# RWKV-7 recurrence on one core: TensorE's turns, low-rank products and opening sum in 64x64 tiles, two factor products on GpSimd, the last inverse level added in PSUM

## The reference

```python
def step(s, inp):
    rt, wt, kt, vt, at, bt = inp
    sa = jnp.einsum('bhvk,bhk->bhv', s, at)
    s = s * wt[:, :, None, :] + sa[..., None] * bt[:, :, None, :] + vt[..., None] * kt[:, :, None, :]
    y = jnp.einsum('bhvk,bhk->bhv', s, rt) if return_y else None
    return s, y
```

## Time and profile before

| | us |
|---|---|
| median of 3 runs (lowest, highest) | 1623.71 (1621.64, 1624.52) |
| the profiled execution's own time | 1622.61 |
| its span | 1620.3 |
| TensorE busy, 14229 matmuls | 1455.2 (90%) |
| VectorE busy | 684.0 (42%) |
| ScalarE busy | 414.0 (26%) |
| GpSimd busy | 194.7 (12%) |
| TensorE's granted clock, mean | 0.957 of full |

### The profile page before, as it was taken

One profiled execution on the slowest core, in us unless ns is written; L12 is line 12 of the kernel. 1 busy time (PEld: TensorE's weight loads), 2 busy tenths in 40 slices (PEclk: granted clock), 3 DMA queues, 4 the chain that ended last, 5 costly groups with the idle time before them and its releaser, 6 DMA issues. The chain is left out here.

```text
span 1620.3 us, 32201 instructions
## 1 busy us (share of the span) xinstructions
PE 1455.2 (90%) x14229; PEld 829.2 (51%) x14229; DVE 684.0 (42%) x1310; ACT 414.0 (26%) x922; POOL 194.7 (12%) x216
## 2 busy tenths in 40 slices
PE   7999999799999998978999997791999988988985
PEld 4445657475554554767788885351333322322331
DVE  3121025554504926756666666286121222221224
ACT  3220135362200004545454553011110000000003
POOL 1100001310001111013333354000000000000000
PEclk9999999999999997989999999895999999999998
DMA  7455430320322111000000000815799999999991
GB/s 274 157 213 205 172 117 2 90 84 14 118 79 78 52 52 52 2 2 4 4 4 5 4 5 2 338 51 202 306 427 426 427 427 427 428 427 428 427 428 75
DMA packets 50731, 285.01 MB, mean 176 GB/s; under 512 B 3993, under 2 KB 7321, under 8 KB 37793
## 3 DMA queue, kind: packets, MB, share of 16 engines
q1 hardware_dynamic: 46592, 266.15, 40.7%
q0 software_dynamic: 2704, 10.18, 1.8%
q10 hardware_dynamic: 1296, 6.62, 1.0%
HBM read 276.63 MB, written 6.29 MB: 175 GB/s over the span
## 5 line engine op out<-in xcount | busy, mean ns | idle before, releaser
L1294 PE MATMUL PS<-arena 128*64 128x512 f32 x336 | 160.3, 632 | 28.7 <-issue 28.7
L1296 PE MATMUL PS<-arena 128*64 128x512 f32 x336 | 156.1, 612 | 0.0
L760 PE MATMUL PS<-arena,ring 128*128 128x512 f32 (+1 forms) x368 | 127.6, 509 | 0.0
L1294 PEld LDWEIGHTS PS<-arena 128*64 128x64 f32 x336 | 47.6, 145 | 130.8 <-issue 130.5
L704 PE MATMUL PS<-ring,arena 128*128 128x512 f32 (+1 forms) x256 | 109.8, 587 | 2.8 <-DMA ring<-w_in 1.5
L1080 PE MATMUL PS<-arena 64*64 64x64 f32 x3776 | 92.9, 224 | 10.8 <-DVE arena L1365 3.9
L798 ACT ACTIVATE arena<-PS 128x512 f32<-128x512 f32 (+3 forms) x76 | 34.7, 485 | 253.4 <-PE PS L760 112.6
L760 PEld LDWEIGHTS PS<-arena,ring 128*128 128x128 f32 x368 | 69.8, 190 | 57.7 <-issue 54.0
L626 DVE TENSOR_REDUCE arena<-PS 128x1 f32<-128x768 f32 (+4 forms) x96 | 62.7, 655 | 82.8 <-PE PS L534 35.4
L1080 PEld LDWEIGHTS PS<-arena 64*64 64x64 f32 x3776 | 77.8, 135 | 24.9 <-issue 9.2
L2387 DVE TENSOR_TENSOR arena<-PS,arena 64x512 f32<-64x512 f32 x32 | 22.0, 689 | 158.4 <-PE PS L1316 158.1
(11 more groups left out here) (361 smaller groups left out, 2609.5 us busy)
## 6 DMA issues: line engine op xcount, KB each, us to landing
arena<-exp_w_gate SPq DMA_DIRECT2D x21, 2048.0 KB, 30.1
arena<-exp_w_up SPq DMA_DIRECT2D x21, 2048.0 KB, 30.0
ring<-exp_w_down SPq DMA_DIRECT2D x20, 2048.0 KB, 31.1
ring<-w_ada SPq DMA_DIRECT2D x12, 2048.0 KB, 12.9
arena<-exp_w_down SPq DMA_DIRECT2D x12, 2048.0 KB, 30.7
ring<-exp_w_gate SPq DMA_DIRECT2D x11, 2048.0 KB, 31.0
ring<-exp_w_up SPq DMA_DIRECT2D x11, 2048.0 KB, 29.5
ring<-w_in SPq DMA_DIRECT2D x9, 2048.0 KB, 14.9
```

Of the source, the lines that this page charges most:

```text
L760: mm = pe.matmul(bank(b, 0, n), u[:, k, (i % 4) * P:(i % 4) * P + P], hT[:, k, t0:t0 + n], start=(k == 0), stop=(k == KT - 1))
L1294: pe.matmul(bank(c, 0, 512, (0, 64)), x, unit(u)[:, k, c * 512:c * 512 + 512], start=(n == 0 and k == 0), stop=(n == 1 and k == 3))
L1296: mm = pe.matmul(bank(c, 0, 512, (64, 128)), x, unit(u + 1)[:, k, c * 512:c * 512 + 512], start=(n == 0 and k == 0), stop=(n == 1 and k == 3))
```

## The change

1. turned() makes 16 matmuls of 64x64 against the 64x64 identity instead of four transposes of 128x128, through the four corners. The row copies bkN change their layout for it.
2. lora: each product of 128 output rows becomes two of 64.
3. The opening: two bf16 matmuls 128x128 by 256 columns become four of 64x64 by 256.
4. al and rt move from VectorE to GpSimd, al ahead of bt, rt ahead of kdk; wc goes to the end of GpSimd's list.
5. xt4 is added onto the turned X in PSUM (bank pair 3) instead of going to bank pair 2. XTf becomes a copy on ScalarE. far goes to bank pair 3, so an waits for Zm4 of the chunk before instead of FT.
6. vN gets a second buffer, and TensorE's, VectorE's and ScalarE's lists have a new order; the loop bodies follow them.

```diff
 SCAN_STEP = {
     "pe": (
-        ("R1b", 0), ("an", 1), ("ab", 1), ("U0", 0), ("tX0", 1), ("Z1", 1), ("U1", 0), ("x1", 1),
-        ("rows", 1), ("Z2", 1), ("tX1", 1), ("dS1", 0), ("dS2", 0), ("x2", 1), ("lora", 2),
-        ("Z3", 1), ("tX2", 1), ("y1", 0), ("x3", 1), ("ak", 1), ("tX3", 1), ("Z4", 1), ("y2", 0),
-        ("vnT", 1), ("y3", 0), ("xt4", 1), ("tL", 1), ("R1a", 1), ("far", 1),
+        ("an", 1), ("ab", 1), ("R1b", 0), ("Z1", 1), ("tX0", 1), ("rows", 1), ("x1", 1), ("U0", 0),
+        ("Z2", 1), ("tX1", 1), ("lora", 2), ("x2", 1), ("vnT", 1), ("U1", 0), ("Z3", 1), ("tX2", 1),
+        ("ak", 1), ("tL", 1), ("x3", 1), ("dS1", 0), ("dS2", 0), ("tX3", 1), ("Z4", 1), ("y1", 0),
+        ("y2", 0), ("y3", 0), ("xt4", 1), ("R1a", 1), ("far", 1),
     ),
     "dve": (
-        ("X0", 1), ("Zm1", 1), ("xa1", 1), ("Zm2", 1), ("xa2", 1), ("Sadd", 0), ("Smul", 0),
-        ("sga", 2), ("Zm3", 1), ("aa", 2), ("ssg", 2), ("xa3", 1), ("scan", 2), ("Zm4", 1),
-        ("Ark", 1), ("Aak", 1), ("yd", 0), ("XTf", 1), ("al", 2), ("FT", 1), ("rt", 2),
+        ("X0", 1), ("Zm1", 1), ("xa1", 1), ("Zm2", 1), ("sga", 2), ("xa2", 1), ("aa", 2), ("ssg", 2),
+        ("Zm3", 1), ("scan", 2), ("xa3", 1), ("Sadd", 0), ("Zm4", 1), ("Aak", 1), ("Ark", 1),
+        ("yd", 0), ("Smul", 0), ("FT", 1),
     ),
     "act": (
-        ("R1", 0), ("AbT", 1), ("U", 0), ("XT0", 1), ("ArbT", 1), ("U1e", 0), ("rowe", 1),
-        ("XT1", 1), ("XT2", 1), ("tsg", 2), ("ta", 2), ("XT3", 1), ("Ei", 2), ("vn", 1), ("ya", 0),
-        ("Ev", 2), ("L", 1), ("kf", 2),
+        ("AbT", 1), ("ArbT", 1), ("R1", 0), ("XT0", 1), ("rowe", 1), ("XT1", 1), ("U", 0),
+        ("tsg", 2), ("vn", 1), ("ta", 2), ("XT2", 1), ("U1e", 0), ("L", 1), ("Ei", 2), ("Ev", 2),
+        ("XT3", 1), ("kf", 2), ("ya", 0), ("XTf", 1),
     ),
     "pool": (
-        ("ArbM", 0), ("bts", 2), ("btk", 2), ("bt", 2), ("wc", 2), ("kdk", 2), ("kd", 2),
+        ("ArbM", 0), ("bts", 2), ("btk", 2), ("al", 2), ("bt", 2), ("rt", 2), ("kdk", 2), ("kd", 2),
+        ("wc", 2),
     ),
...
             def opened_by_unit():
 
-                for q in range(2):
-                    lo = pcol(2, q, 0)
-                    pe.matmul(PS[:, lo:lo + 256], unit_half, rep(outweigh_half, 4), start=True, stop=True,
-                              skip_group_check=True)
-
-            def turned(b, half, src, opens=True):
-
-                for d in range(2):
-                    for j2 in range(2):
-                        lo = pcol(b, d, half) + j2 * P
-                        mm = pe.matmul(PS[:, lo:lo + P], src(d, j2), ident, is_transpose=True, start=(opens and j2 == 0), stop=True,
-                                       skip_group_check=True)
+                for c in range(2):
+                    for r in range(2):
+                        lo, rows = pcol(2, r, 0), slice(r * 64, r * 64 + 64)
+                        pe.matmul(PS[c * 64:c * 64 + 64, lo:lo + 256], unit_half[rows, rows],
+                                  rep(outweigh_half[rows, :], 4), start=True, stop=True, skip_group_check=True)
+
+            def turned(b, half, src, frm, to):
+
+                begun = set()
+                for j, q, d in heads(frm, to):
+                    r = half_other(frm, j, q)[0]
+                    i, o = half_other(to, j, q)
+                    lo = pcol(b, o, half) + (2 * d + j // 2) * 64
+                    mm = pe.matmul(PS[i * 64:i * 64 + 64, lo:lo + 64], src(d, j, q),
+                                   C("ident2", 0, 64, (r * 64, r * 64 + 64)),
+                                   start=(o, i) not in begun, stop=True, skip_group_check=True)
+                    begun.add((o, i))
                 return mm
...
-                        pe.matmul(bank(0, c, 64), lora[0:64, d, j * P:j * P + P], wal[0:64, tok:tok + 64],
-                                  start=True, stop=True)
-                        mm = pe.matmul(bank(1, c, 64), lora[64:128, d, j * P:j * P + P], wal[64:128, tok:tok + 64],
-                                       start=True, stop=True)
+                        for h in range(2):
+                            lo, to = j * P + h * 64, (h * 64, h * 64 + 64)
+                            pe.matmul(bank(0, c, 64, to), lora[0:64, d, lo:lo + 64], wal[0:64, tok:tok + 64],
+                                      start=True, stop=True)
+                            mm = pe.matmul(bank(1, c, 64, to), lora[64:128, d, lo:lo + 64], wal[64:128, tok:tok + 64],
+                                           start=True, stop=True)
...
-                    signal(product(2, 0, A, A, split(W["Z"], A), whole(W["XT"], A), by_direction=True), "xt4", near)
...
+                    signal(product(3, 0, A, A, split(W["Z"], A), whole(W["XT"], A), clear="no"), "xt4", near)
...
+                if runs("al", ahead):
+                    needs(pool, ("Ei", ahead), ("an", ahead - 3), ("ak", ahead - 3), ("R1b", ahead - 3))
+                    signal(removal(pool, ahead), "al", ahead)
```

More of the change, by code:

```diff
@@ L68 @@
  FINAL) = range(17)
-N_SCAN = 27
+N_SCAN = 28
 LIVES = [
@@ L1138, in rwkv_pe @@
                 now, near, ahead = g, g + 1, g + 2
-                if runs("R1b", now):
-                    needs(pe, ("R1a", now), ("al", now), ("Smul", now - 1))
-                    signal(product(1, 0, A, A, al_of(now), split(W[f"S{now % 2}"], A), clear="no"), "R1b", now)
                 if runs("an", near):
-                    needs(pe, ("al", near), ("bt", near), ("FT", near - 1))
+                    needs(pe, ("al", near), ("bt", near), ("Zm4", near - 1))
                     opened_by_unit()
@@ L1172, in rwkv_pe @@
                     needs(pe, ("xa1", near), ("XT0", near))
-                    signal(turned(3, 0, pairs_of(W["X"])), "tX1", near)
-                if runs("dS1", now):
-                    needs(pe, ("rowe", now), ("vn", now), ("U1e", now))
-                    signal(product(1, 0, B, A, row_op(now, 1), whole(W["vN"], B), clear="bank"), "dS1", now)
-                if runs("dS2", now):
-                    needs(pe, ("U1e", now))
-                    signal(product(1, 0, B, A, row_op(now, 0), split(W["U"], B), clear="no"), "dS2", now)
+                    signal(turned(3, 0, whole(W["X"], B), B, A), "tX1", near)
+                if runs("lora", ahead):
+                    needs(pe, ("rowe", ahead - 1))
+                    signal(lora_products(ahead), "lora", ahead)
                 if runs("x2", near):
@@ L1182, in rwkv_pe @@
                     signal(product(2, 0, A, B, whole(W["XT"], A), split(W["Z"], A)), "x2", near)
-                if runs("lora", ahead):
-                    needs(pe, ("rowe", ahead - 1))
-                    signal(lora_products(ahead), "lora", ahead)
+                if runs("vnT", near):
+                    needs(pe, ("XT1", near))
+                    signal(turned(3, 0, values_of(near), A, B), "vnT", near)
+                if runs("U1", now):
+                    needs(pe, ("U", now), ("FT", now))
+                    signal(product(1, 1, B, B, split(W["FT"], B), split(W["U"], B), clear="no"), "U1", now)
                 if runs("Z3", near):
@@ L1410, in rwkv_dve @@
                     needs(dve, ("x1", near), ("X0", near))
[L1411 removed]
+                    x = of_blocks(W["X"])
                     signal(dve.tensor_tensor(x, x, pair4(2), ALU.add), "xa1", near)
@@ L1445, in rwkv_dve @@
                     signal(running_sums(), "scan", ahead)
+                if runs("xa3", near):
+                    needs(dve, ("x3", near), ("xa2", near))
+                    x = of_blocks(W["X"])
+                    signal(dve.tensor_tensor(x, x, pair4(2), ALU.add), "xa3", near)
+                if runs("Sadd", now):
+                    needs(dve, ("dS2", now), ("y1", now - 1), ("Smul", now - 1))
+                    signal(dve.tensor_tensor(both(f"S{(now + 1) % 2}"), both(f"S{now % 2}"), pair(1, 0), ALU.add), "Sadd", now)
                 if runs("Zm4", near):
@@ L1842, in _ @@
                     signal(act.activation(both("R1"), pair(1, 0), ACT.Copy), "R1", now)
-                if runs("AbT", near):
-                    needs(act, ("ab", near), ("Z4", near - 1), ("tL", near - 1))
-                    signal(act.activation(W["AbT"].rearrange("p (s q n) -> p q s n", q=2, n=64), pair_wide(0, 0), ACT.Copy), "AbT", near)
+                if runs("XT0", near):
+                    needs(act, ("tX0", near), ("xt4", near - 1))
+                    signal(act.activation(of_blocks(W["XT"]), pair4(3), ACT.Copy), "XT0", near)
+                if runs("rowe", near):
+                    needs(act, ("rows", near), ("dS2", near - 2))
+                    for a in range(2):
+                        ins = act.activation(of_blocks(row_half(near, a)), pair4(0, a), ACT.Copy)
+                    signal(ins, "rowe", near)
+                if runs("XT1", near):
+                    needs(act, ("tX1", near), ("x1", near))
```

(22 more changed lines are left out.)

224 lines of the change are left out of this document (103 added, 121 removed).

## The result

| | before | changed |
|---|---|---|
| median (lowest, highest), us | 1624.12 (1621.64, 1625.65) | 1695.5 (1694.29, 1696.61) |
| profiled execution's own time / its span | 1622.61 / 1620.3 | 1696.6 / 1694.8 |
| ratio, with its 95% interval | | 1.0436 (1.0423 to 1.0448) |
| TensorE busy, granted clock | 1455.2, 0.957 | 1443.5, 0.953 |
| VectorE, ScalarE, GpSimd busy | 684.0, 414.0, 194.7 | 653.3, 420.9, 212.0 |

The prediction was 1597 us, in a range of 1588 to 1611: wrong in sign. TensorE's busy time does fall by 12 us over the launch, and yet the launch takes 71 us more.

The account below looks back on a forecast made before the run. TensorE's work was taken to bound the recurrence: -27.1 us from first opening to last R1b and +0.5 at the start, -26.6 from 1622.6, gave 1596.0; with 1.1 for the median, 1597 us, range 1588 to 1611.

Parts of the forecast that it names:

- TensorE is the bound: Recurrence, 725 to 980 us: TensorE is busy 239 of 255 us at full clock, so its work sets the time.
- The prices of the array work: TensorE, latent step: a turn 0.52 for 0.70 us, low-rank products 1.04 for 2.04; 2.35 us less work in all.
- The rival of the 1.00 turn: Turns overlapping at two corners only cost 1.00 us each, 46 us above the sum: 1643 us; chance 0.07.
- the 0.87: Turn price in us if column tiling excludes the f32 transpose mode; 34 us above the sum, 1631 us.
- So 20.1 against 22.5: Recurrence: each of six latent steps takes 20.1 us instead of 22.5, 2.4 us less.
- The walk: New order laid on TensorE operation by operation with operand waits: latent step 20.1 us, context step 18.5.
- instructions arrive too slowly: Rival, recurrence: TensorE wants about 97 instructions a microsecond; if it got only 80, 1638 us; chance 0.03.
- the row against it: 907.8 to 918.5 us: 69 instructions a microsecond with TensorE busy 10.4 of 10.7 us, cited against slow instruction arrival.
- the 14.9 us of "issue" on L1080: 70 stalls on TensorE in the kernel before, cited for the rival of slow instruction arrival.
- The first rival: GpSimd or VectorE operands come 0.5 to 1.2 us late each step: +6 to +14 us, 1603 to 1611; chance 0.14.
- The order: TensorE's new order in a latent step leaves waits of 0.47 us before Z2 and 0.3 before far.
- I am wrong if ... 'issue' idle time grows by more than 10 us: Sign of failure on TensorE, beside turns over 0.8 us or TensorE waiting for GpSimd.

Follow-up runs that it names:

- a3: Changed kernel with 128x128 transposes, wide low-rank products and two-matmul opening put back; new order, GpSimd's al and rt, xt4 in PSUM stay: 1641.94 us, ratio 1.0088.
- a4: a3 plus seven f32 matmuls of 512 columns to an unused bank ahead of the first opening: 1637.29 us, ratio 1.0073 to the kernel before.
- c2: Kernel before with 256 already satisfied semaphore waits written for each step on SyncE: 1623.2 us, ratio 0.999.
- c1: Kernel before with 32 already satisfied semaphore waits written at eight places of a step on TensorE: 1709.56 us, ratio 1.0538.
- d1: Kernel before with 126 one-column bf16 matmuls added to each step on TensorE, into unused PSUM columns: 1659.61 us, ratio 1.0228.
- b2: Kernel before with seven f32 matmuls of 512 columns to an unused bank ahead of the first opening: 1626.35 us, ratio 1.0013.
- b3: Kernel before with only al and rt moved to GpSimd, in the changed kernel's order there: 1625.31 us, ratio 1.001.

## Why the prediction was wrong

**"TensorE is the bound": half right.** The array was busy 94% of the recurrence. But the instruction supply stood right behind it, at 21.4 us a latent step against 22.5, and was not costed as a bound of its own. By the 3.7 us a step could take an estimated 778 matmuls in its 22.5 us before its supply took over; the change asked for 996.

**The prices of the array work: right.** TensorE's timeline of the changed kernel, where no block ends:

```profile
915.89 1.62 PE L1125 MATMUL PS<-arena 64*64 64x64 f32 x96
...
920.39 0.69 PE L1104 MATMUL PS<-arena 64*64 64x64 f32 x32 [0.31 <-DVE arena L1423]
920.90 0.65 PE L1125 MATMUL PS<-arena 64*64 64x64 f32 x32
921.37 0.23 PE L1153 MATMUL PS<-arena 64*64 64x64 f32 x2
```

Three turns (tX0 and the double rows) take 915.89 to 917.36, 0.49 each, and tX1 at 920.90 takes 0.47; I had 0.52. The rival of the 1.00 turn is out, and so is the 0.87 worked out from the Trainium skill's rule on the transpose mode (TensorEngine Tiling, Restrictions and Gotchas; TensorE: Matmul & The Clock Gate, Terms) as a price of the turn. The low-rank products take 0.99 in the six steps in which no block ends within them (1.04 predicted). The opening takes 0.1 to 0.2 (0.2 predicted). Busy time falls by 1.3 us a latent step where I had work falling by 2.35 from 21.65; busy time overlaps rows, so the two are not the same measure.

**"So 20.1 against 22.5": this is the step that failed.** The walk let TensorE take its next instruction whenever array and operand were free. Whether the instructions themselves had arrived was a term that it put at nothing. The runs put in its place the larger of that walk and (instructions of the step)/256 x 3.7 us, and block by block rather than over the step, as a3 shows. For a latent step 7.8 x 3.7 = 29, measured 27.3 to 31.4, 29.1 on average; for a context step with 900 matmuls 7.06 x 3.7 = 26.1, measured 25.1 to 26.3.

**The rival "instructions arrive too slowly" was the mechanism, with 0.03.** Three errors made it small. Its price was taken at 80 a microsecond, from no row, between 69 and 97; at the measured 69 its 22,000 instructions take 319 us for 260, which gives about 1682. And the row against it was read the wrong way: "371 matmuls and 370 loads in 10.7 us, 69 a microsecond, with TensorE busy 10.4" was no proof of room above 69. It is the very rate at which blocks came in the changed kernel (68.5 from first opening to last). And the 14.9 us of "issue" on L1080 were not what they were taken for: 13.1 of them stand before weight loads, and only 1.8, 6 times, before matmuls.

**GpSimd.** al and rt take 1.37 us a pair, not 1.8 (22 at 683 ns, 16 at 686), and GpSimd holds nothing up but the first opening, by 0.9 us where 0.5 was predicted; the other 1.8 of the +2.7 stand ahead of the recurrence. Its busy time rose by 17 us, not 36: al and rt add 26.5 where 36 were priced, and the others got shorter, wc above all (8.5 to 3.8 us for 24 copies) and btk and kdk (43.2 to 40.2). VectorE's fell by 31, not 38. The first rival, gain given back through late operands, did not happen in the changed kernel: the waits for VectorE that remain are 4.1 us before Z2 and 4.0 before xt4, about what the walk had (0.47 a step, and 1.0 in four context steps).

**The order.** By itself it was to close waits; in a3 and a4 it does not gain and loses 17 and 13 us. Part of it is supply again (denser stretches, no credit), part stays open as said above.

**"I am wrong if ... 'issue' idle time grows by more than 10 us"** was the right thing to look at: it grew by 70.

## What to carry to other kernels

Count TensorE's instructions in each stage, not only its array time. In this case small f32 products ran at about 69 matmuls and loads a microsecond on average at most (256 in 3.7 us); cutting a turn of four 128x128 transposes into 64x64 products takes eight times the instructions, here 32 matmul rows for 4. By that figure, an estimate, a stage that already runs at 62 to 66 has 5 to 10% of room, however short each instruction is. Waits named "issue" in the middle of a product, 127 or 128 matmuls apart, are the sign of it, also when there are few of them.

## What the runs showed of the hardware that was not expected

- TensorE's instructions come in packets of 16 KB, 256 instructions, on q8; starts never lie closer than 3.2 us in any run, with a median of 3.74 in the changed kernel, though a packet itself takes about 1.1 us. TensorE goes on about 1.4 us after a packet's end, and the next packet starts about 1.2 us after that. Three times the traffic on the other instruction queue, q14, changed nothing (c2).
- There is no credit: a kernel whose mean demand is below the supply (a3) still stops up to 1.5 us at block ends in its dense stretches.
- A wait that is already met costs TensorE 55 ns (c1); a one-column bf16 matmul with its load in a 64x64 tile about 8 ns (18 in 0.15 us, d1).
- The granted clock fell to half around the end of the low-rank products, where the wait for the first opening begins (716.6 us in the kernel before, 719.3 in a3), and it stayed there for 10.2 us in the kernel before and 27.3 in a3. With warming matmuls in that wait it was 3.4 (b2), and the time hardly moved.
- The 24 copies of wc on GpSimd took 383 ns each in the kernel before and 191 in the changed one and in b3, where al no longer runs on VectorE and wc stands last in GpSimd's list. Which of the two did it was not tried.
